# Mixture-of-experts blocks of a two-block layer stack: the second block's gate and up product, its slot's next weight loads, a divided listing, and a peeled last pair

## The reference, cut to what matters

```
def _hierarchical_moe(x, w_rg, b_rg, w_re, b_re, w_gate, w_up, w_down):
    g_logits = xf @ w_rg + b_rg                      # 4 groups
    g_w, g_idx = top_k(softmax(g_logits), 1)
    e_logits = (xf @ w_re + b_re) of the chosen group  # 8 experts in each, 32 in all
    e_w, e_idx = top_k(softmax(e_logits), 2)
    # each of 512 x 2 assignments gets a row in a block of its expert
    ...
    def expert_block(args):
        xb, e = args
        h = jax.nn.silu(xb @ w_gate[e]) * (xb @ w_up[e])
        return h @ w_down[e]
    y_rows = lax.map(expert_block, (x_rows, block_e))
    y = segment_sum(y_rows * row_gate, row_tok)       # back to the tokens
```

## Time and profile before

| | us |
|---|---|
| median of three runs | 3282.34 |
| the profiled execution, its own time | 3289.94 |
| its span, first to last instruction | 3288.1 |
| busy: PE / DVE / ACT / POOL | 3023.3 / 1157.1 / 857.4 / 473.1 |
| PE, gate and up products L2977, x1856 | 450.0 |
| PE idle before these, most of it ended by DMA `slot<-in_moe_w_up` | 62.0, of it 53.2 |
| PE, down products L2994, x960 | 218.9 |

### The profile page before, as it was taken

One profiled execution on the slowest core, in us unless ns is written; L12 is line 12 of the kernel. 1 busy time (PEld: TensorE's weight loads), 2 busy tenths in 40 slices (PEclk: granted clock), 3 DMA queues, 4 the chain that ended last, 5 costly groups with the idle time before them and its releaser, 6 DMA issues. The chain is left out here.

```text
span 3288.1 us, 43221 instructions
## 1 busy us (share of the span) xinstructions
PE 3023.3 (92%) x16807; PEld 2151.9 (65%) x16807; DVE 1157.1 (35%) x1833; ACT 857.4 (26%) x1691; POOL 473.1 (14%) x662
## 2 busy tenths in 40 slices
PE   7998989999999999999898999999789899998985
PEld 6777767778777887887677744444378676444442
DVE  3562764233344333436554500000173365000002
ACT  2423751232223330113461111111121242111111
POOL 0031530000000000000071011111122331111111
PEclk9998999999999999999898999999899999999997
DMA  4242012133333323232002789999843117999996
GB/s 131 90 108 78 2 52 90 40 89 90 102 90 90 102 83 97 96 102 77 15 1 91 282 364 397 430 430 427 328 135 106 55 34 305 379 429 430 428 426 257
DMA packets 240091, 604.72 MB, mean 184 GB/s; under 512 B 39646, under 2 KB 181340, under 8 KB 215261
## 3 DMA queue, kind: packets, MB, share of 16 engines
q1 hardware_dynamic: 228060, 583.05, 47.4%
q0 software_dynamic: 10560, 16.27, 1.3%
q10 hardware_dynamic: 1344, 3.67, 0.5%
HBM read 595.56 MB, written 24.16 MB: 188 GB/s over the span
## 5 line engine op out<-in xcount | busy, mean ns | idle before, releaser
L2977 PE MATMUL bank<-slot,moe_xT 128*64 128x512 f32 x1856 | 450.0, 641 | 62.0 <-DMA slot<-in_moe_w_up 53.2
L2977 PEld LDWEIGHTS bank<-slot,moe_xT 128*64 128x64 f32 x1856 | 154.3, 148 | 314.6 <-issue 301.0
L3071 DVE TENSOR_TENSOR ex_h<-ex_gate,bank 64x512 f32<-64x512 f32 x64 | 44.1, 690 | 868.4 <-ACT ex_gate L3034 868.4
L263 PE MATMUL bank<-hT_hi,cut_lo 128*128 128x512 f32 x1248 | 308.2, 389 | 0.0
L263 PE MATMUL bank<-hT_hi,ahead 128*128 128x512 f32 x624 | 249.9, 400 | 20.8 <-DVEq L471 13.1
L263 PEld LDWEIGHTS bank<-hT_hi,cut_lo 128*128 128x128 f32 x1248 | 234.3, 188 | 48.7
L263 PE MATMUL bank<-hT_lo,ahead 128*128 128x512 f32 x624 | 247.9, 397 | 0.0
L263 PE MATMUL bank<-hT_hi,cut_hi 128*128 128x512 f32 x624 | 243.4, 390 | 3.0 <-DVE cut_hi L292 3.0
L263 PE MATMUL bank<-hT_lo,cut_hi 128*128 128x512 f32 x624 | 242.8, 389 | 0.0
L2994 PE MATMUL bank<-slot,ex_hT 128*64 128x512 f32 x960 | 218.9, 596 | 2.3 <-ACT ex_hT L3038 2.3
L3034 ACT ACTIVATE ex_gate<-bank 64x512 f32<-64x512 f32 x64 | 37.9, 592 | 499.1 <-PE bank L2977 499.1
(11 more groups left out here) (580 smaller groups left out, 5300.9 us busy)
## 6 DMA issues: line engine op xcount, KB each, us to landing
slot<-in_moe_w_gate SPq DMA_DIRECT2D x60, 2048.0 KB, 16.9
slot<-in_moe_w_up SPq DMA_DIRECT2D x60, 2048.0 KB
slot<-in_moe_w_down SPq DMA_DIRECT2D x60, 2048.0 KB
raw<-in_w_in SPq DMA_DIRECT2D x26, 1024.0 KB, 5.4
raw<-in_w_ffn_in SPq DMA_DIRECT2D x44, 512.0 KB, 4.9
raw<-in_ssd_w_in SPq DMA_DIRECT2D x20, 1024.0 KB, 5.2
raw<-in_attn_w_qkv SPq DMA_DIRECT2D x18, 1024.0 KB, 5.0
raw<-in_w_in SPq DMA_DIRECT2D x24, 512.0 KB, 4.3
```

Of the source, the lines that this page charges most:

```text
L263: last = nc.tensor.matmul(out, a(pa, k), b(pb, k), start=(begins and late == "hi" and k == 0 and n == 0), stop=(ends and late == "lo" and ...
L2977: last = nc.tensor.matmul(GU[s][rows, :], xT[:, s, k * ER:(k + 1) * ER], raw[slot][which][:, k * HID:(k + 1) * HID], start=(k == 0), stop= ...
L3071: nc.vector.tensor_tensor(h[:, s, :], gate[:, s, :], GU[s][right, :], ALU.mult).then_inc(h_ready, 1)
```

## The change

Line numbers of the changed kernel differ from those above.

- The router's biases get a place of their own beside the router's weights, and their two loads are issued with those, in the preceding stage.
- In `moe_route` the gate and up product of block 1 is done at the end of PE's work, behind the listing and `turn(1)`; behind it SP issues G4 and U4 into slot 1. The listing is divided: 4 of its 8 products ahead of `turn(1)`, 4 behind it. The filler is 34 products in place of 26. POOL's clearing of `moe_x` and `moe_y` and its two empty scatters wait for `placed`. ACT has one more small operation, a Silu, behind the two exponentials.
- In `moe_experts` PE begins with `turn_h` of block 0; SP begins with D3.
- POOL's `scatter` copies the column of `place` before it waits for y, behind a wait for the scatter before it in the same buffer.
- The loops of SP and PE over pairs end one pair earlier, and the last pair is written out. In it, G31 and U31 are loaded in halves (first half of each, then second half of each), and PE multiplies the first halves (`last_gate_up`) before it waits for the second ones. The numbers of blocks that this needs are read from three more words of `pairs`.

```diff
 class Router:
+        self.bias = nc.alloc_sbuf_tensor_at(f"router{layer}_bias", [EG + NE, 1], F32, offset=first - ROUTER_BIAS)
...
     def loads(self, sp):
...
+        sp.dma_start(self.bias[0:EG, :], column(A.moe_b_router_group_2[layer])).then_inc(self.bias_loaded, 16)
+        sp.dma_start(self.bias[EG:, :], column(A.moe_b_router_expert_2[layer])).then_inc(self.bias_loaded, 16)
...
@@ moe_route, sync
-                sp.dma_start(br[0:EG, :], column(A.moe_b_router_group_2[layer])).then_inc(loaded, 16)
-                sp.dma_start(br[EG:NL, :], column(A.moe_b_router_expert_2[layer])).then_inc(loaded, 16)
...
                 sp.wait_ge(first_gate_up, 1)
                 K.slots.load(sp, 0, 3, (GATE, UP))
+                sp.wait_ge(first_gate_up, 2)
+                K.slots.load(sp, 1, 4, (GATE, UP))
                 sp.wait_ge(x_stored, 32)
@@ moe_route, gpsimd
+                pool.wait_ge(placed, 1)
                 for s in range(2):
                     nc.gpsimd.memset(x[:, s, :], 0.0)
@@ moe_route, tensor
-                keep_running(nc, K, 26)
+                keep_running(nc, K, 34)
...
                 gather(1, range(2, TT)).then_inc(first_gathered, 1)
                 pe.wait_ge(placed, 1)
-                for n in range(2 * TT):
...
+                list_rows(range(TT))
                 pe.wait_ge(rows_kept, 2)
                 turn(1).then_inc(first_turned, 1)
+                list_rows(range(TT, 2 * TT)).then_inc(listed, 1)
+                gate_up(1).then_inc(first_gate_up, 1)
@@ moe_route, scalar
-                act.wait_ge(loaded, 32)
-                nc.scalar.activation(lgT[:, :], K.bank[0][0:NL, :], ACT.Identity, bias=br[:, :]).then_inc(biased, 1)
+                act.wait_ge(K.router.bias_loaded, 32)
+                nc.scalar.activation(lgT[:, :], K.bank[0][0:NL, :], ACT.Identity, bias=K.router.bias[:, :]).then_inc(biased, 1)
...
+                nc.scalar.activation(g4[:, :, 1, :], g4[:, :, 0, :], ACT.Silu)
@@ moe_experts, sync
                 for b in range(4, AROUND):
-                    first(b)
+                    if b > 4:
+                        first(b)
                     load(b - 1, (b - 1) % 3, DOWN, down_ready, b - 3)
-                with sp.Fori(AROUND // 2, n) as i:
+                with sp.Fori(AROUND // 2, pairs_but_one(sp)) as i:
...
+                e = named(n * 2 - 1)
+                sp.wait_ge(gate_up_ready, but_two)
+                for part, steps in enumerate(parts(KD)):
+                    for which in (GATE, UP):
+                        words = slice(steps[0] * HID, (steps[-1] + 1) * HID)
+                        sp.dma_start(raw[1][which][:, words], weights_d[which][ds(e, 1)].rearrange("e p f -> p (e f)")[:, words]).then_inc(
+                            w_loaded[1 + part][which], 16)
+                load(named(but_two), 0, DOWN, down_ready, but_three)
                 load(named(n * 2 - 1), 1, DOWN, down_ready, but_two)
@@ moe_experts, gpsimd
-                def scatter(s, b):
-
-                    pool.wait_ge(y_kept, b + 3)
+                def scatter(s, i, b):
+                    pool.wait_ge(y_stored[s], i * 16 + 16)
                     nc.gpsimd.tensor_copy(to[:, s:s + 1], place[:, ds(b, 1)]).then_inc(directed, 1)
                     pool.wait_ge(directed, b + 1)
+                    pool.wait_ge(y_kept, b + 3)
@@ moe_experts, tensor
+                def last_gate_up(b, loaded):
+                    pe.wait_ge(x_kept, b + 2)
+                    for part, steps in enumerate(parts(KD)):
+                        for which in (GATE, UP):
+                            pe.wait_ge(w_loaded[1 + part][which], 48 if part else loaded)
+                        for k in steps:
+                            for which, rows in ((GATE, left), (UP, right)):
+                                last = nc.tensor.matmul(GU[1][rows, :], xT[:, 1, k * ER:(k + 1) * ER], raw[1][which][:, k * HID:(k + 1) * HID],
+                                                        start=(k == 0), stop=(k == KD - 1))
+                    last.then_inc(gate_up_ready, 1)
...
-                pe.sem_inc(gate_up_ready, 1)
+                pe.sem_inc(gate_up_ready, FIRST)
...
-                gate_up(1, 0, 1, 16)
                 turn_h(0, 0)
```

72 lines of the change are left out of this document (49 added, 23 removed).

## The result

The changed kernel took 3294.70 us (median of 7 runs, 3284.98 to 3298.01), the kernel before 3285.74 (7 runs, 3281.25 to 3287.78): ratio 1.0027, 95% interval 1.0018 to 1.0037, so 9.0 us slower (5.9 to 12.2). The forecast of 3286.4 was too low by 8.3. Of that 3.4 is the base (I had the median of three runs, 3282.34), and 4.9 the shift: +9.0 for my +4.1. The time is in the range, and on the side of the slower case, to which I had given 0.33.

What follows compares the result with a forecast made beforehand. PE's chain was taken to bound each layer up to G8's issue, then a fixed amount of bytes and a tail. Layer 0's +2.4 and layer 1's +1.7 made +4.1 on 3282.34: 3286.4 us, range 3273 to 3297.

Steps and rivals of the forecast that it cites:

- The frame: Each layer: PE's chain counts up to G8's issue, then fixed bytes, then a tail; time moves by G8's shift plus tail.
- Move of the product, cover lost: Routing to experts: from E, block 0's product end, block 1's product no longer covers scaling, copy and gather; turn_x 5.3 later.
- The landing: Block 2's gather, issued behind G4 and U4, lands 8.8 us later, at E (block 0's product end) + 25.9.
- the rival of the early landing: Block 2's gather lands within 4 us despite the queued weights; 3272.9 us, chance 0.16.
- The clock in the seam: PE idles around the expert stage's start, so turn_x and block 2's product slow: 1.5 us a layer, bounds 0 and 2.9.
- the seam: Stretch from block 0's product end to block 2's turn_x, with work moved across the barrier; +6.1 us a layer forecast.
- the sum of the gains: Savings forecast from biases, clearing, filler, scatter and halves over both layers: 9.5 us.
- Biases and clearing: Start of routing: earlier bias loads give 0.15 us, clearing moved off a small DVE operation 0.75; 0.9 a layer.
- The longer filler: Routing: more filler keeps the clock for the counting; 1.4 us gained in layer 0, layer 1's whole front gains 0.9.
- Scatter: POOL's column copy ahead of y: 0.7 us a layer ahead of G8, 1.0 a layer at the last scatter.
- Halves: Layer tails: G31 and U31 in halves let PE start earlier; 0.4 us in layer 0, 2.5 in layer 1.
- The full-price rival: The slower case: gather lands after 9.8 us and PE pays 2.9 of half clock; +12.5, 3294.8 us, chance 0.33.

Runs made afterwards that it cites:

- e9: The changed kernel with POOL issuing the gathers of blocks 2 and 3 at the end of routing, ahead of G4 and U4; 3290.00 us, ratio 1.0009.
- e3: The changed kernel with G4 and U4 issued only in the expert stage, once block 2's gather has landed; 3284.01 us, ratio 1.0000.
- e1: The changed kernel with block 1's product and G4/U4 back in the expert stage and the listing whole ahead of the turn; 3280.51 us, ratio 0.9990.
- e2: The kernel before with only block 1's product and G4/U4 moved into routing and the listing divided; 3295.85 us, ratio 1.0034.
- e8: The kernel before with only POOL's new scatter order, the column copied while y is awaited; 3283.39 us, ratio 0.9995.
- e5: The kernel of e1 with 40 filler products in place of 34; 3272.98 us, ratio 0.9959 to the kernel before.
- e7: The kernel of e1 without halves: last pair back in the loop, G31 and U31 whole; 3284.04 us, ratio 0.9997 to the kernel before.
- e6: The kernel of e5 with 5 filler products behind the turn of block 1 in routing; 3272.77 us, ratio 0.9961 to the kernel before.
- e12: The kernel before with the change's routing front (early biases, later clearing, extra Silu) and 40 filler products; 3276.72 us, ratio 0.9975.
- e11: The changed kernel with 40 filler products in place of 34 and nothing else; 3285.43 us, ratio 1.0003 to the kernel before.
- e4: The changed kernel with filler products of the identity put where PE idles around the start of the expert stage; 3301.39 us, ratio 1.0053.
- e10: The kernel before with 44 filler products in place of 26 in routing and nothing else; 3281.84 us, ratio 0.9992.

## Why the prediction was partly right

*The frame* held in all 14 profiles: the time follows G8 (113 to 129 us behind the start), while the rest varies by 5.3 at most.

*Move of the product, cover lost.* Right: the stage opens at E + 14.2 (worked out 13.8), the gather is issued at 17.4 (17.1), `turn_x` begins at 26.1 and 26.8 (25.9). But I had PE's own chain too short, at 21.6, since I costed down at 3.65. With the clock lost it ends at 24.5 and 24.9 (e9). So the gather behind the weights leaves only 1.7 and 2.2 of idleness beyond it, not 4.3. To take away the gather's wait alone gains no more than that; e3 gained the rest by the earlier opening and the quicker down.

*The landing.* 8.5 and 9.2 for the 8.8 taken; e3 shows the cause, 3.0 and 3.6 when G4 and U4 come behind. The Trainium skill, DMA: Bandwidth & Descriptors, "SWDGE vs HWDGE vs iDMA", says that each DMA engine takes turns between the queues that the two kinds of issuer feed. The landings here do not bear it out: 7.9 to 9.2 in the eight places where the gather stands 4.6 to 5.1 us behind G4, 4.7 to 5.7 where it stands 8.1 us or more behind G3 and ahead of G4 (e9), 3.0 and 3.6 with no weights just ahead (e3). They go by the bytes issued ahead of the gather, and the rival of the early landing did not come.

*The clock in the seam*, 1.5 a layer: 0 in layer 0, 2.0 in layer 1, so 1.0 as a mean and inside the bounds. The larger loss of clock was in down, which I had put under the gather's cover.

So gather and clock, 6.8 a layer and 13.6 in all, were measured as 11 to 12 (e1, e2). **What failed is the sum of the gains**: I had 9.5 (the seam's 0.7 a layer for the scatter among them), and e1, which has them all and no seam, 3.3 (0.3 to 6.2). The seam came out some 2 below its 13.6, the gains some 6 below theirs; the time stayed in the range because the range was wide enough for both, and not because the sum was right. By terms, against before's execution:

- *Biases and clearing*, 0.9 a layer: 0.80 in both. Right, and by the parts too (layer 0): DVE's first copy comes 0.06 earlier (0.15), the small operation takes 0.17 in place of 0.91 (0.75).
- *The longer filler*, 1.4 in layer 0; in layer 1 a front of -0.9 in all. Layer 0 gave 1.6 up to G3 beside the biases. In layer 1 G3 came 0.41 later than before, 1.3 worse than I had, and outside the bound. The step that failed is "the counting began only as they ended". That was one execution of before, whose filler ran slowly (8.56); in e2 and e8, with the same front, it took 6.07 and ended 1.8 and 2.1 short of the counting. And I did not ask where 34 fillers end when they start earlier and at full clock. They end 1.4 us short, PE idles, and the clock falls within the counting. Against e2 and e8 the front of layer 1 gains 2.5, as layer 0's does, so the loss of 0.41 is against a lucky execution. e5 shows what was to be had: with 6 more fillers the counting keeps the clock in both layers, and the time is 5 to 15 us lower. The sign set down for a filler without effect, 6 us of counting in layer 0, nearly came: it takes 5.4, and 3.4 in e5.
- *What the front wins goes on*: assumed without a word. e1's seam is 1.2 to 1.5 longer than before's, because block 1's product is slow (9.73 and 10.03). That is 2.7 of the missing gain.
- *Scatter*, 0.7 + 1.0 a layer: too large. I had read the 0.86 behind the copy as the copy's landing. It stays when the copy is long done: y's copy ends at 2370.99, the scatter goes out at 2371.85, again 0.86. It belongs to the issue behind a wait, whichever the wait is. Left are 0.33 at the end, so the 1.0 a layer there was too large by 0.7. e8's time, -1.6 (-4.6 to +1.6) for my -3.4, does not settle what the scatter gives ahead of G8.
- *Halves*, 0.4 and 2.5: 0.4 and 2.3 (e7 against e1). Right, and as thought: with halves block 31's product of layer 1 begins 369.8 behind G8 without a wait, before it waited until 371.2.

Of what was to be seen: G4 at 12.8 (13), `turn_x` waiting for DMA (1.7 and 2.2, not 3 to 5, since down filled the rest), G8 2.9 later in layer 0 (3 to 4), share 1.01 behind it; but the stretch without transfers ahead of G8 was not longer in either layer (about 3.5 us; before 3.5 to 4), and the last scatter's issue is not directly behind y but 0.86 after it. The full-price rival gave 3294.8, by chance the measured time: it had the seam at 9.2 and gains of 5.9, and the base 3.4 too low.

Open stays why the medians differ by 9.0 and the profiled executions by 5.3. The one of before lay 4.2 above its median; its counting in layer 1 (14.90) was quicker than in e2 and e8 (16.74 and 16.84), whose front is the same. Such draws of the clock, 2 to 3 us a stage, are in the executions of most kernels here. They bound what rows can tell: from start to picked rows e1's execution gains 7.9 on before's, by the medians it is 3.3. Whether a front that keeps the clock also makes the runs lie closer is not shown: e5, e6 and e12 lie within 6.3, 1.5 and 4.4 us (5, 5 and 10 runs), but e11 within 9.4 (11 runs), and e2, which does not keep it, within 4.0 (6 runs).

## What to carry to other kernels

Before work is moved ahead of a barrier, list what it covered behind it: here 7 us of matmul hid a scaling, a copy and a gather, and moving it gained PE nothing and opened them all. Issue small gathers ahead of large loads that nobody needs soon. Fit a filler to the wait that it covers for the clock that it will run in, and fit it again after each change that moves its start; that, not the moved work, was the best change here.

## What the runs showed of the hardware

- With PE idle for 1.4 to 2.2 us ahead of the counting, a chain of small products, the clock fell in 15 of the 17 places where the profiles have it, and the counting took 4.8 to 6.1 us; in the changed kernel, layer 0, the granted clock was 0.57 over its stretch. In the other two (layer 0 of e3 and e4) it took 3.4. With no idleness ahead of it, it took 3.3 to 3.4 in all 11 places. So the idleness decides most often but not alone.
- After 1.0 us of idleness the filler ran at full clock in all 20 places (e5: 80 records in 9.2). After 2.8 to 3.2 us it did so in six of eight, and not in layer 1 of before (52 records in 8.6) and of e10 (88 in 12.6).
- POOL sat idle for 0.8 to 0.9 us ahead of a gather or scatter of a block, whatever it had waited for last: a copy of a column 0.2 long, or y. A gather that followed another directly, without a wait, came after 0.31 (e9).
- A gather issued 4.6 us behind 4 MB of weights landed after 8.5 us, the same gather with no weights just ahead after 3.0 (e3).
- A product of two 128x128 f32 operands is two records, 0.23 us in all at full clock.
